# One level of Strassen's scheme in the down projection of a hybrid encoder layer

## The reference

```python
def conv_ffn(h, w_up, conv_w, conv_b, w_down):
    z = h @ w_up                                   # (512, 1024) @ (1024, 5632)
    S = z.shape[1]
    zp = jnp.pad(z, ((0, 0), (CONV_W - 1, 0), (0, 0)))
    zc = conv_b
    for j in range(CONV_W):
        zc = zc + zp[:, j:j + S] * conv_w[j]
    a, u = jnp.split(zc, 2, axis=-1)
    return (jax.nn.silu(a) * u) @ w_down           # (512, 2816) @ (2816, 1024)
...
x = x + conv_ffn(rms_norm(x, norm_ffn_g[l]), w_up[l], conv_w[l], conv_b[l], w_down[l])
...
return rms_norm(x, final_norm_g)
```

## Time and profile before

| | |
|---|---|
| median of 3 runs | 965.3 us |
| span of the profiled execution | 963.6 us |
| outside the span (median less span) | 1.7 us |
| PE busy | 951.7 us |
| DVE, ACT, POOL busy | 563.3, 390.9, 34.6 us |
| moved by DMA | 93.8 MB, 31.4% of 16 engines' time |
| up projection, from the profile | 603 to 835.2 us |
| down projection with the residual | 835.2 to 958.5 us |
| after the last matmul | 5.1 us |

### The profile page before, as it was taken

The page is one execution under the profiler, slowest core; times in us unless marked ns, Lnnn a source line. Parts: engine busy times, 40 slices in busy tenths (PEclk is TensorE's granted clock), DMA queues, the critical chain, the costliest instruction groups (busy, mean ns, idle before and its releaser), DMA issues.

```text
span 963.6 us, 12000 instructions
## 1 busy us (share of the span) xinstructions
PE 951.7 (99%) x4782; PEld 796.8 (83%) x4782; DVE 563.3 (58%) x646; ACT 390.9 (41%) x427; POOL 34.6 (4%) x27
## 2 busy tenths in 40 slices
PE   8999999999999999999999999999999999999997
PEld 6899889777888788888888878888888888888886
DVE  5877654554677564466545548776777677711123
ACT  6473223332664552333333446444434444311122
POOL 1000000200000000000021005000000000000000
PEclk9999999999999999999999999999999999999999
DMA  7414212122232523333223224343333432222212
GB/s 253 160 44 131 73 59 88 46 79 62 66 95 81 178 76 97 98 98 120 90 91 126 79 75 131 88 127 92 87 87 104 113 87 87 92 103 111 88 44 88
DMA packets 121570, 93.80 MB, mean 97 GB/s; under 512 B 3930, under 2 KB 115902, under 8 KB 121406
## 3 DMA queue, kind: packets, MB, share of 16 engines
q1 hardware_dynamic: 121534, 93.27, 31.4%
HBM read 91.16 MB, written 2.10 MB: 97 GB/s over the span
## 4 chain that ended last, share of the span: by engine, by line
PE 91%; DVE 4%; ACT 3%; issue 1%; DMA 0%; SPq 0%; DVEq 0%; ACTq 0%
PE ps L496 66%; PE ps L999 12%; PE ps L860 5%; DVE wL L1345 1%; PE ps L540 1%; PE ps L640 1%; PE ps L631 1%; PE ps L624 1%; ACT wH L1029 1%; PE ps L874 1%; PE ps L890 1%; ACT L1029 1%; PE ps L646 1%; DVE hgF L1345 0%; DVE hgG L1537 0%
## 5 line engine op out<-in xcount | busy, mean ns | idle before, releaser
L496 PE MATMUL ps<-hH,wH 128*128 128x512 f32 x784 | 308.5, 394 | 4.1 <-DVE wL L1345 3.8
L496 PE MATMUL ps<-hH,wL 128*128 128x512 f32 x784 | 305.3, 389 | 0.0
L496 PE MATMUL ps<-hL,wH 128*128 128x512 f32 x784 | 305.2, 389 | 0.0
L1345 DVE TENSOR_TENSOR wL<-raw,wH 128x2048 fp32r<-128x2048 f32 (+3 forms) x90 | 188.4, 2094 | 130.9 <-ACT wH L1029 130.7
L1029 ACT ACTIVATE wH<-raw 128x2048 fp32r<-128x2048 f32 (+3 forms) x90 | 157.7, 1752 | 227.5 <-PE ps L496 146.3
L496 PEld LDWEIGHTS ps<-hH,wH 128*128 128x128 f32 x784 | 147.2, 188 | 37.9 <-DVE wL L1345 5.6
L496 PEld LDWEIGHTS ps<-hH,wL 128*128 128x128 f32 x784 | 147.1, 188 | 31.0
L496 PEld LDWEIGHTS ps<-hL,wH 128*128 128x128 f32 x784 | 147.2, 188 | 30.0 <-issue 0.2
L999 PE MATMUL ps<-wH,actH 128*128 128x512 f32 x176 | 68.7, 390 | 0.0
L999 PE MATMUL ps<-wH,actL 128*128 128x512 f32 x176 | 68.5, 389 | 0.0
L999 PE MATMUL ps<-wL,actH 128*128 128x512 f32 x176 | 68.5, 389 | 0.0
(11 more groups left out here) (275 smaller groups left out, 1225.4 us busy)
## 6 DMA issues: line engine op xcount, KB each, us to landing
raw<-in_w_in SPq DMA_DIRECT2D x57, 512.0 KB, 4.1
raw<-in_w_up SPq DMA_DIRECT2D x44, 512.0 KB, 4.6
raw<-in_w_down SPq DMA_DIRECT2D x22, 512.0 KB, 3.9
raw<-in_w_branch SPq DMA_DIRECT2D x24, 256.0 KB, 4.3
raw<-in_w_out SPq DMA_DIRECT2D x8, 512.0 KB, 4.1
raw<-in_w_mkv SPq DMA_DIRECT2D x8, 512.0 KB, 4.4
xtok<-in_x SPq DMA_DIRECT2D x8, 256.0 KB, 4.4
xtok<-in_x SPq DMA_DIRECT2D x1, 2048.0 KB, 9.1
```

The source lines that it names most:

```text
L496: last = pe.matmul(out_ap, a, b, start=start and k + m == 0, stop=stop and m == 2 and k == len(terms) - 1)
L1345: q.sig(dve.tensor_tensor(out_ap, a, b, op), sem)
```

## The change

The down projection is written as one level of Strassen's scheme (in Winograd's form). Tokens, channels and output columns are each halved. Channel tile i (0 to 10) and tile i+11 form **pair i**. Each pair takes 7 products of half size (256 tokens x 128 channels x 512 columns) in place of 8: seven operands of activations and seven of weights, of which some are sums.

- **Sums of the activations.** `ffn` writes its product into `pair[:, i, ...]`. After the second tile of a pair DVE makes four sums of 128 x 256 (`act_sums`). The split into upper and lower parts (`sH`, `sL`) is moved from `ffn` to the down projection.
- **Sums of the weights.** POOL issues transfers from `w_down` to two tensors in HBM (`t123`, `t4`), some copying and some adding onto what is there. They are issued in 14 rounds; a round starts when all transfers of earlier rounds have landed and PE has reached a given slot: rounds 0 to 7 when slots 2 to 9 are finished, rounds 8 to 13 when slots 17 to 22 are. Rounds 3 to 10 have 4 copies and 4 additions of 256 KB each. There are 88 transfers.
- **Order on PE.** The first four products of all pairs are made first (24 matmuls a pair), then the other three (18 a pair). The last two pairs are done together so that the parts of the output end one after another. Between the halves of the work ACT copies one product out of PSUM (`m1`), DVE makes sums of products (`uu`, `uv`, `otok`), and the residual is added at that point, again by 32 transposes.
- **Splits.** ACT and DVE split both the activations and the weights for each pair: 3 x 1024 columns in the first part, 768 + 1024 + 512 in the second.
- **Last pair** (pair 10 of the second part) is loaded and split in its own third set of buffers, spread over steps 5 to 7 of the second part.
- **End.** The norm works on quarters of the output in SBUF. ACT squares quarters, DVE and POOL share the multiplication by the gain, ACT and SP the stores.

The diff, cut to its core, in the order of the file: the buffers, then SP, POOL, PE (first part, second part, the last two pairs), ACT, and DVE (turn from up to down, and the end).

```diff
+        pair = at("pair", A, [P, NP, 7, HT])
+        order = [(g, k) for g in range(NP + 5) for k in range(3)]
+        for k in range(3):
+            order += [(NP + 5 + k, j) for j in range(3)] + [(LAST, k)]
+        order += [(g, k) for g in range(NP + 8, LAST) for k in range(3)]
+        nth = {part: i + 1 for i, part in enumerate(order)}
...
+            def load_down(i):
+                n = Slot(N_DN + i)
+                if i < 2:
+                    sp.wait_ge(lo_ready, n.n(-1))
+                else:
+                    sp.wait_ge(d_lo, nth[i - 2, 2])
...
+                sp.dma_start(raw[n.s][:, 0:S], w_down[0, rows, 0:S]).then_inc(raw_in[n.s], 16)
+                sp.dma_start(raw[n.s][:, S:4 * S], t123[rows].rearrange("p q c -> p (q c)")).then_inc(raw_in[n.s], 16)
...
+            for i in range(2):
+                load_down(i)
+            sp.wait_ge(slot_done, N_DN)
             sp.dma_start(gainF[:, :], final_norm_g.partition_broadcast(P)).then_inc(g_row, 16)
...
+            def weight_sums(r):
...
+                if r:
+                    pool.wait_ge(t_sum, 16 * (4 * made[0] + 2 * made[1] + made[2] + made[3]))
+                if r < NP:
+                    a, b = rows(r)
+                    pool.dma_start(t123[a, 1, :], w_down[0, a, 0:S]).then_inc(t_sum, 16)
+                    pool.dma_start(t123[a, 2, :], w_down[0, a, S:D]).then_inc(t_sum, 16)
+                    pool.dma_start(t123[a, 0, :], w_down[0, b, S:D]).then_inc(t_sum, 16)
+                    pool.dma_start(t4[a, :], w_down[0, b, 0:S]).then_inc(t_sum, 16)
+                if 0 <= r - 1 < NP:
+                    a, b = rows(r - 1)
+                    pool.dma_start(t123[a, 1, :], w_down[0, a, S:D], accum_op=ALU.add).then_inc(t_sum, 16)
+                    pool.dma_start(t123[a, 2, :], w_down[0, b, S:D], accum_op=ALU.add).then_inc(t_sum, 16)
+                if 0 <= r - 2 < NP:
+                    a, b = rows(r - 2)
+                    pool.dma_start(t123[a, 0, :], t123[a, 1, :], accum_op=ALU.add).then_inc(t_sum, 16)
+                if 0 <= r - 3 < NP:
+                    a, b = rows(r - 3)
+                    pool.dma_start(t4[a, :], t123[a, 0, :], accum_op=ALU.add).then_inc(t_sum, 16)
+
+            for r in range(8):
+                pool.wait_ge(slot_done, 3 + r)
+                weight_sums(r)
             for h in range(1, H):
                 pool.wait_ge(hg_sq, h + 1)
...
+            for i in range(NP):
+                for q, b in enumerate((4, 6, 2, 0)):
+                    if q % 2 == 0:
+                        pe.wait_ge(d_lo, nth[i, 1 + q // 2])
+                    if i == 0 and q >= 2:
+                        pe.wait_ge(taken, N_DN - 3 + q)
+                    last = half_product(i, q, b, i == 0, i == NP - 1)
...
+            for i in range(NP - 2):
+                g = NP + i
+                for q, b in enumerate((4, 6, 0)):
+                    if i == 0:
...
+                        residual((2, 3) if q == 2 else (0, 1), range(4, 8) if q == 1 else range(4), b)
+                    pe.wait_ge(d_lo, nth[g, 1 + q // 2])
+                    last = half_product(g, q, b, False, False)
...
+            for q, b in ((0, 4), (2, 0), (1, 6)):
+                for t in range(2):
+                    for g in (LAST - 1, LAST):
+                        pe.wait_ge(d_lo, nth[LAST - 1, 1 + q // 2])
+                        last = half_product(g, q, b, False, g == LAST, (t,))
+                    last.then_inc(d_sum, 1)
...
+            def down_weights(i):
+                n = Slot(N_DN + i)
+                act.wait_ge(raw_in[n.s], n.loads())
+                if i < 2:
+                    act.wait_ge(slot_done, n.n(-1))
+                for c in (0, D):
+                    upper(i, wH[n.s][:, c:c + D], raw[n.s][:, c:c + D])
...
+            ffn(Slot(N_DN - 2), NP - 1, 0, lambda: both(0))
+            down_lower(1)
+            ffn(Slot(N_DN - 1), NP - 1, 1, lambda: down_weights(1))
+            for i in range(2, NP):
+                both(i)
+                if i == 4:
+                    act_sums(NP - 1)
...
+            dve.wait_ge(o_sum, 5)
+            inverse(2)
+            q.settle()
+            scaled(2, 0, D, o_fin)
+            dve.wait_ge(o_sum, 6)
+            inverse(3)
+            for t in range(2):
+                dve.wait_ge(d_sum, 10 + t)
+                added(t, 6, uv, 1, ALU.subtract, d_out)
+            q.settle()
+            scaled(3, 0, S, o_fin)
+            for t in range(2):
+                dve.wait_ge(o_sum, 7 + t)
+                inverse(t)
+                q.settle()
+                scaled(t, S, D, o_fin)
```

More of the change, by code:

```diff
@@ L467, in _, with rows @@
                 pool.memset(att[i][:, :, :], 0.0).then_inc(att_zero, 1)
+            def weight_sums(r):
+                def rows(i):
+                    return slice(P * i, P * i + P), slice(FF // 2 + P * i, FF // 2 + P * i + P)
+                made = [min(max(r - back, 0), NP) for back in range(4)]
+                if r:
[19 more added lines that the diff above has]
+                weight_sums(r)
             for h in range(1, H):
@@ L1003, in down, with half_product @@
+            def half_product(g, q, b, start, stop, tiles=(0, 1)):
+                s = home(g)
+                for t in tiles:
+                    ah, al = (x[s][:, q, P * t:P * t + P] for x in (sH, sL))
+                    for m, (x, w) in enumerate(((ah, dwH), (ah, dwL), (al, dwH))):
+                        last = pe.matmul(ps[:, b + t, :], x, w[s][:, S * q:S * q + S], start=start and m == 0,
+                                         stop=stop and m == 2, skip_group_check=True)
                 return last
@@ L1300, in ffn, with upper, down_upper @@
                 tap(1)
-                hi(n + 2)
-                act.wait_ge(f_prod, n.n(1 - N_UP))
-                do(actH[:, bass.ds(n.n(-N_UP), 1), :], prod[:, :], ACT.Copy, f_hi)
+                after()
+            def upper(g, dst, src):
+                do(dst, src, ACT.Copy, d_hi)
+            def down_upper(i):
+                n = Slot(N_DN + i)
+                act.wait_ge(f_sum, 4 * i + 4)
+                if i >= 2:
+                    act.wait_ge(d_done, i - 1)
+                upper(i, sH[n.s][:, :, :], pair[:, i, 0:4, :])
@@ L1330, in _ @@
[L1330 to L1337 removed]
+            ffn(Slot(N_DN - 2), NP - 1, lambda: down_upper(0))
+            down_weights(0)
@@ new lines, in _ @@
+            for i in range(NP - 1):
+                lower_upper(i)
+                if i == 0:
+                    act.wait_ge(d_sum, 1)
+                    do(m1[:, :, :], ps[:, 4:6, :], ACT.Copy, d_m1)
+                if i == 4:
+                    act.wait_ge(d_out, 5)
+                    for t in (2, 3):
+                        square_of(t, 1, o_sum)
+                    do(ostat[:, 0, 5:6], eps[:, 0:1], ACT.Sqrt)
+                if 5 <= i < 8:
+                    last_upper(i - 5)
@@ L1340, in _ @@
+            for t in range(2):
+                act.wait_ge(o_inv, 7 + t)
+                act.wait_ge(d_gain, 2 + t)
+                do(otok[:, t, 0:S], g11[:, t, :], ACT.Copy, o_act, scale=ostat[:, t, 3:4])
+            act.wait_ge(o_fin, 4)
+            act.dma_start(out[0, P:2 * P, S:D], otok[:, 1, S:D]).then_inc(out_done, 16)
         @block.vector
@@ new lines, in rest, with down_lower, down_weights @@
+            def rest(dst, src, up):
+                tt(dst, src, up.bitcast(F32), ALU.subtract, d_lo)
+            def down_lower(i):
+                dve.wait_ge(d_hi, nth[i, 0])
+                s = home(i)
+                rest(sL[s][:, :, :], pair[:, i, 0:4, :], sH[s][:, :, :])
+            def down_weights(i):
+                s = home(i)
+                for k in range(2):
+                    dve.wait_ge(d_hi, nth[i, 1 + k])
+                    c = slice(D * k, D * k + D)
+                    rest(wL[s][:, c], raw[s][:, c], wH[s][:, c])
@@ L1903, in _, with lower_lower @@
+            def lower_lower(i, parts=range(3)):
+                g = NP + i
+                s = home(g)
+                for k in parts:
+                    dve.wait_ge(d_hi, nth[g, k])
+                    if k == 0:
+                        rest(sL[s][:, 0:3, :], pair[:, i, 4:7, :], sH[s][:, 0:3, :])
+                    else:
+                        c = slice(0, D) if k == 1 else slice(D, D + S)
+                        rest(dwL[s][:, c], draw[s][:, c], dwH[s][:, c])
             q.sig(dve.memset(za[:, 0:2], 0.0))
@@ new lines, in part, with inverse, scaled, added @@
+            def part(tiles, c):
+                for t in tiles:
+                    ts(ostat[:, t, 4:5], ostat[:, t, c:c + 1], 1.0 / D, EPS, ALU.mult, ALU.add, sem=o_inv)
+            def inverse(t):
+                q.sig(dve.reciprocal(ostat[:, t, 3:4], ostat[:, t, 2:3]), o_inv)
+            def scaled(t, a, b, sem):
+                stt(otok[:, t, a:b], otok[:, t, a:b], ostat[:, t, 3:4], gainF[:, a:b], ALU.mult, ALU.mult, sem)
```

(17 more changed lines are left out.)

316 lines of the change are left out of this document (194 added, 122 removed).

## The result

| | before | after |
|---|---|---|
| median of 4 runs each, same chip | 965.36 us (965.15 to 966.38) | 958.32 us (957.15 to 958.64) |
| ratio, 95% interval | | 0.9923 (0.9909 to 0.9938) |
| span of the profiled execution | 963.6 us | 956.5 us |

What follows compares the result with a forecast made beforehand. PE was taken as the bound, busy 951.7 of 963.6 us. Terms -15.0 + 1.9 + 0.3 + 2.0 = -10.8 gave 952.8 for the profiled execution and, with 1.7 to the median, 954.5 us; range 950.8 to 960.5.

Steps and rivals of the forecast that it cites:

- 66 matmuls fewer: Down projection on PE: 462 matmuls in place of 528, at 0.2268 us each, 15.0 us less.
- pace of the 462 that stay: Down projection on PE: shape unchanged, so each remaining matmul was priced at the earlier 0.2268 us.
- turn: From up to down projection: DVE's sums and splits delay pair 1's weights, so PE waits 1.9 us.
- other waits of the down projection: Steps of its first and second parts: no wait in the first, 0.3 us (0 to 3) in the second.
- end: After the last matmul: DVE's queue makes it 1.6 us later, four stores add 0.4; +2.0 (0.5 to 4).
- weight sums: POOL's transfers beside the early slots: they cost PE nothing, with POOL free at 147, before hgsq needs it by 180.1.
- the forecast's own case: Whole kernel: the summed terms give 954.5 us, with its own range 952.5 to 957 and 58% chance.
- side traffic: Rival, slots 3 to 23: longer loads, lo and hi make PE wait 0.2 us in each of 20; +4, 958.5 us; 15%.
- R: Time of a full round of eight weight-sum transfers, taken as 14 us; above 19.4 PE would stall in slot 12.

Runs made afterwards that it cites:

- e5: The changed kernel with sH and sL moved to a multiple of 512 bytes from the weights; 955.01 us, ratio 0.9893.
- e2: The kernel before with the down projection's activations and all tiles behind them 64 bytes further on in SBUF; 968.75 us, ratio 1.0031.
- e10: e8 without the weight sums, SP loading other weights of the same size in their place; 954.9 us, ratio 0.9894.
- e8: e5 with ffn of slots 55 and 56 and the first sums written out ahead of the loop on ACT and DVE; 953.76 us, ratio 0.9879.
- e6: The kernel before with 64 bytes of padding between hL and raw, moving the weights and all tiles behind them together; 978.67 us, ratio 1.0135.
- e1: The kernel before with its down projection changing PSUM bank every 3 matmuls instead of 6; 966.2 us, ratio 1.0003.
- e9: The kernel before with the down projection's activations and what lies behind them 256 bytes further on; 966.2 us, ratio 1.0.
- e11: e8 with eight more copies of 256 KB in each of rounds 0 to 10; 1000.75 us, ratio 1.0363.

## Why the prediction was right and wrong

| term | forecast | measured | how it is known |
|---|---|---|---|
| 66 matmuls fewer | -15.0 | -15.0 | 462 in the trace, at 0.2268 each |
| pace of the 462 that stay | 0 | +3.0 | e5 against after; e2 |
| turn | +1.9 (0 to 3) | +0.45 | trace |
| other waits of the down projection | +0.3 (0 to 3) | +0.25 | trace |
| end | +2.0 (0.5 to 4) | +2.2 | trace |
| weight sums | 0 | 0 | e10 against e8 |
| first `ffn` of the up projection | not seen | +1.1 | trace; e8 (-1.25) |
| before the up projection | 0 | +0.9 | trace |
| sum | -10.8 | -7.1 | |

The time of 958.3 lies inside the stated range (950.8 to 960.5), but outside the 952.5 to 957 of the forecast's own case. It came there by a term that the forecast had at nothing, the pace, with a smaller turn and a missed start of the up projection beside it. The upper part of the range was there for "side traffic", which e10 rules out, so that the range held is in part luck.

**Count right; the end right in size, not in its path.** The forecast let DVE's queue decide and had ACT done before it. The chain after goes through ACT (start, us, what):

```profile
947.27 1.29 DVE otok L1537
...
948.67 0.73 ACT otok L1146
...
951.58 1.32 ACT otok L1146 x2
```

ACT scales a quarter of another token tile at 948.67, beside the last matmuls, then has twice about 1.1 us for square, sum and root, which I had counted, and behind them its own two scalings, 1.32 us together, which I had not set against DVE. It ends at 952.90, 3.8 us after the last matmul's end (949.11). DVE's last row, against the earlier trace rows:

```profile
951.90 0.75 DVE L1537 SCALAR_TENSOR_TENSOR otok<-otok,ostat,gainF 128x512 f32<-128x512 f32 x1
```

ends at 952.65, 3.5 after it, where I had 4.3. (My own terms for this queue, from -0.2 on, add up to 3.8 and not to the 4.1 written there; with the hand-overs 4.0.) From 952.90 to the span's end it is 3.6 us, against the 2.46 + 0.4 of the forecast: a store of 256 KB takes 2.5 to 3.1 us to land among four, where the earlier trace rows has 2.1. The two errors, -0.5 and +0.7, nearly cancel.

**The failed step: "The shape stays 128x128 by 512 columns" and 0.2268 us is "what one more costs".** The count was priced by the rate of other tiles in another place, and then "nothing else runs beside PE that could take this back except by a wait" closed the question. The shape does stay; the distance in SBUF between what PE holds and what it streams doesn't, and e2, e5 and e6 show that this is the whole of the slower pace: 64 bytes off costs 6.6 ns a matmul, 3.0 us here, of which e5 wins back 2.5 (the rest turns into waits). Of the Trainium skill, "SBUF — State Buffer", section "SBUF: two separate sides", says that on the engines' side only the shared pair of ports causes contention, and that PE never waits for anyone. It gives no reason for a pace that depends on where two of PE's own tiles lie; the runs show that it does (226.7 against 233.3 ns). Whether this is contention at all, no run here shows.

**The turn: a term sized too large.** DVE's queue is as forecast, but each hand-over in it was shorter. (At the good pace PE is earlier and the turn costs 0.6, by the gaps in e5's trace; 1.9 is too large there too.) The timeline of DVE after, against the earlier trace rows:

```profile
834.76 0.69 DVE L1530 TENSOR_TENSOR za<-ps,rstd_row 128x512 f32<-128x512 f32 x1
836.33 1.54 DVE L1537 SCALAR_TENSOR_TENSOR ca<-za,par,ca 128x512 f32<-128x512 f32 x2 [0.89 <-ACT ca L1146]
837.79 0.68 DVE L1530 TENSOR_TENSOR zu<-ps,rstd_row 128x512 f32<-128x512 f32 x1
...
841.61 2.35 DVE L1530 TENSOR_TENSOR wL<-raw,wH 128x1024 fp32r<-128x1024 f32 x2
```

`za` to the convolution is 1.57 us (1.82 in the earlier trace rows), the convolution 1.54 (1.65), `zu` to the weights 3.82 (4.12). The rows that I took them from lie in a loop, whose instructions take their addresses from registers; these slots are written out. That this is the reason is shown for slots 55 and 56 (e8) and taken over for these. The forecast's 841.4 for the weights would be 843.4 here, since the program is 2.0 later at this point; they come at 841.61. Of these 1.8 us, 0.7 lie between `za` and the weights, as named, and 1.0 lies before `za`, in slot 75's and in the four splits (4.5 us instead of 4.8). PE waited 0.2 us, and with the restart 0.45 is lost.

**What I missed: the same effect at the other end.** Slots 55 and 56 were written out before and are in the loop now. Before, from `za` to the weights of slot 57:

```profile
608.01 0.69 DVE L1345 TENSOR_TENSOR za<-ps,rstd_row 128x512 f32<-128x512 f32 x1
609.60 1.54 DVE L1352 SCALAR_TENSOR_TENSOR ca<-za,par,ca 128x512 f32<-128x512 f32 x2 [0.89 <-ACT ca L1029]
...
614.89 2.29 DVE L1345 TENSOR_TENSOR wL<-raw,wH 128x2048 fp32r<-128x2048 f32 x1
```

and after:

```profile
609.11 0.69 DVE L1530 TENSOR_TENSOR za<-ps,rstd_row 128x512 f32<-128x512 f32 x1 [0.22 <-DVE rstd_row L1977]
610.96 1.66 DVE L1537 SCALAR_TENSOR_TENSOR ca<-za,par,ca 128x512 f32<-128x512 f32 x2 [1.16 <-ACT ca L1146]
616.77 2.28 DVE L1530 TENSOR_TENSOR wL<-raw,wH 128x2048 fp32r<-128x2048 f32 x1
```

6.88 us became 7.66 there, and with what comes before `za` the weights are 1.0 later, for which PE waits 0.8 at 618. e8 writes the two out again and wins 1.25 us on e5 by the medians, 1.0 by the spans of the profiles.

**The weight sums: right, with R well placed.** The forecast took 14 us for a round. POOL's timeline (rounds 3 to 7, then the additions):

```profile
85.85 0.56 POOL L545 DMA_DIRECT2D t<-in_w_down  x1 [8.18 <-DMA t<-t]
101.35 0.56 POOL L545 DMA_DIRECT2D t<-in_w_down  x1 [9.98 <-DMA t<-t]
117.93 0.56 POOL L545 DMA_DIRECT2D t<-in_w_down  x1 [11.06 <-DMA t<-t]
133.32 0.56 POOL L545 DMA_DIRECT2D t<-in_w_down  x1 [9.84 <-DMA t<-t]
147.31 0.56 POOL L545 DMA_DIRECT2D t<-in_w_down  x1 [8.47 <-DMA t<-t]
...
151.05 1.81 POOL L558 DMA_DIRECT2D t<-t  x1
174.04 6.87 POOL L567 TENSOR_TENSOR hgsq<-hgsq 128x512 f32<-128x512 f32 x3 [21.18 <-ACT hgsq L1146]
```

Rounds take 14.0 to 16.6 us, set by their transfers and not by the gates as I had it; POOL is free at 153 and its additions start when ACT delivers, 0.9 late only because the whole execution is. The Trainium skill, "Collectives: The Full Stack", on why reduce-scatter is slower (an adding transfer at half the rate), led to an estimate of 13.7, near the shortest of these rounds; that the halved rate is the reason isn't shown by it (landing takes 5.1 us for the copies and 8.9 for the additions, 1.7 times as long). The trap "DVE blocks DMA" of the Trainium skill, "SBUF — State Buffer", was not seen: the eight issues of a round follow each other at 0.53 us with DVE busy 0.6 of the time. The forecast had taken DVE's whole busy share for it, where that trap is told of its two-port modes alone. So "side traffic" (958.5) was not the way to the time near 958: e10 rules it out.

**The 0.9 before the up projection** goes with the dip of the clock at 11 to 15 us. e1 and e9, versions of the kernel before that do the same work up to 835 us, have it too, and end the up projection 1.0 and 1.2 later than it. The window of e1, and then of e9:

```profile
6.00:17.00 11.00, 8.20 (x37) 6.39 (x35) 8.74 (x24) 7.75 (x13) 0.00 (x0) 0.84 1.01 326
6.00:17.00 11.00, 8.94 (x37) 7.16 (x37) 8.69 (x25) 7.75 (x13) 0.00 (x0) 0.84 1.04 328
```

The profiles of before and of e2 to e8 don't have it. So it belongs to an execution and not to the change, and it fits the two times about 1.2 us apart at which runs of one kernel lie (965.2 and 966.4 for before). What brings it about stays open: just ahead of it, from 8 to 11 us, PE was busy for 1.17 us in the changed kernel's profile and for 0.90 in that of before, where the clock stayed full. Without it the difference of the two profiles is 8.0 us, and the changed kernel's runs show both kinds too (957.15, and 958.29 to 958.64).

## What to carry to other kernels

Matmul counts must be priced at the pace of the tiles that the new code will use, and that pace depends on addresses: for float32 matmuls like these lay stationary and streamed tiles whole multiples of 256 bytes apart, and when a stage's layout changes, compare the time between matmul starts in the two traces before looking for waits. If a chain passes through DVE or ACT at the edge of a loop, a turn written out ahead of the loop or behind it can be shorter than one in it. The transfers that build operands inside HBM were free here as long as their rounds left the issuing engine before its next urgent work (e8 against e10) and cost 47 us when they didn't (e11); work out that deadline, because the rounds ahead of it add up.

## What the runs showed of the hardware that was not expected

- Matmuls of 128x128 by 512 columns of float32, at full clock, start 226.7 ns apart when streamed and stationary tile lie a multiple of 256 bytes apart, 233.3 at 64 bytes off and 232.4 at 128. Why, and why 128 is nearly as bad as 64, no run here shows. After a restart even aligned ones run unevenly, at 224 to 236, for some three to ten matmuls (before at 843.9 us, e5 at 841.7).
- An `ffn` written out goes from `za` to its convolution, through ACT, 0.25 us faster than one in a loop (1.57 against 1.82; 1.58 in e8 against 1.85 in the changed kernel). For the first two slots together it is 1.0 us by the profiles of e8 and e5, 1.25 by their medians.
- Transfers of 256 KB inside HBM, issued by POOL, take 0.53 us to issue; in rounds of eight, copies land 5.1 us after their issue and additions 8.9. At times POOL shows 8 to 9 us between two issues with no wait and no work (9.10 at 291.76 in the changed kernel, 8.29 in e11). The cause of the gaps stays open. With eight more copies a round the DMA engines were 0.93 busy between 49 and 190 us (e11).
